# The experts' inner width in three parts (1024, 1024, 768 columns) in place of four quarters of 704

## What is computed

```python
def expert_choice_ffn(h, w_router, w_gate, w_up, w_down):   # D_MODEL 1024, EXPERT_FF 2816, N_EXPERTS 16
    ...
    cap = CAPACITY_FACTOR * n // N_EXPERTS                  # 32 tokens of one group, 64 of the other
    aff = jax.nn.softmax((t @ w_router).astype(jnp.float32), axis=-1)
    gate, idx = lax.top_k(aff.T, cap)
    def expert(args):
        wg, wu, wd, ix, g = args
        xe = t[ix]
        he = jax.nn.silu(xe @ wg) * (xe @ wu)
        return (he @ wd) * g[:, None].astype(he.dtype)
    ...
    y = jnp.zeros((n, D), h.dtype).at[idx.reshape(-1)].add(ye.reshape(-1, D))
```

## Time and profile before

| | us |
|---|---|
| median of 3 runs | 2247.36 |
| the profiled execution's own time | 2247.78 |
| its span, first to last instruction | 2246.0 |
| TensorE busy in the span | 2154.8 (96%) |
| VectorE busy | 1586.4 (71%) |
| ScalarE busy | 1373.0 (61%) |
| weight loads (PEld) recorded busy | 1873.9 (83%) |

### The profile page before, as it was taken

The page is one execution under the profiler, slowest core; times in us unless marked ns, Lnnn a source line. Parts: engine busy times, 40 slices in busy tenths (PEclk is TensorE's granted clock), DMA queues, the critical chain, the costliest instruction groups (busy, mean ns, idle before and its releaser), DMA issues.

```text
span 2246.0 us, 30582 instructions
## 1 busy us (share of the span) xinstructions
PE 2154.8 (96%) x11924; PEld 1873.9 (83%) x11924; DVE 1586.4 (71%) x1264; ACT 1373.0 (61%) x1118; POOL 180.5 (8%) x140
## 2 busy tenths in 40 slices
PE   6989979999995999999999999999999999999997
PEld 5857868888775898999988899898998989999896
DVE  5375334223447888888888888888888888888885
ACT  4364335222224677776777767677776777777774
POOL 1202200000013000010100101010010100101000
PEclk9999979999996999999999999999999999999999
DMA  5110142112415999999999999999999999999994
GB/s 228 57 56 25 57 134 70 62 57 113 162 67 205 362 380 353 386 365 370 375 368 372 367 378 374 367 377 365 378 366 375 369 358 391 359 373 372 366 382 173
DMA packets 71582, 623.99 MB, mean 278 GB/s; under 512 B 8336, under 2 KB 8720, under 8 KB 18800
## 3 DMA queue, kind: packets, MB, share of 16 engines
q1 hardware_dynamic: 63264, 595.62, 68.7%
q0 software_dynamic: 7840, 27.40, 4.3%
q10 hardware_dynamic: 432, 0.34, 0.0%
HBM read 609.70 MB, written 13.63 MB: 278 GB/s over the span
## 4 chain that ended last, share of the span: by engine, by line
PE 86%; DVE 5%; ACT 3%; issue 3%; DMA 2%; POOL 0%; ACTq 0%; DVEq 0%; POOLq 0%
PE PS L492 26%; PE PS L494 26%; PE PS L493 26%; DVE x_w_low L1114 2%; ACT x_w_high L1047 2%; PE PS L589 2%; PE PS L574 1%; PE PS L833 1%; PE PS L602 1%; PE PS L501 1%; DVE hidden L1465 1%; DMA bias_windows<-in_bias_prompt 1%; DVE s L1221 0%; ACT w_high L852 0%; PE PS L700 0%
## 5 line engine op out<-in xcount | busy, mean ns | idle before, releaser
L1114 DVE TENSOR_TENSOR x_w_low<-x_w_raw,x_w_high 128x2816 fp32r<-128x2816 f32 (+1 forms) x382 | 1176.6, 3090 | 244.0 <-ACT x_w_high L1047 242.4
L1047 ACT ACTIVATE x_w_high<-x_w_raw 128x2816 fp32r<-128x2816 f32 (+2 forms) x384 | 978.7, 2557 | 251.8 <-PE PS L494 212.0
L492 PE MATMUL PS<-x_w_high,xT_high 128*96 128x352 f32 x2048 | 667.9, 326 | 1.4 <-DVE xT_low L1114 1.4
L494 PE MATMUL PS<-x_w_high,xT_low 128*96 128x352 f32 x2048 | 660.7, 323 | 0.0
L493 PE MATMUL PS<-x_w_low,xT_high 128*96 128x352 f32 x2048 | 658.3, 321 | 0.0
L492 PEld LDWEIGHTS PS<-x_w_high,xT_high 128*96 128x96 f32 x2048 | 330.7, 161 | 6.8 <-issue 4.4
L493 PEld LDWEIGHTS PS<-x_w_low,xT_high 128*96 128x96 f32 x2048 | 332.9, 163 | 2.4
L494 PEld LDWEIGHTS PS<-x_w_high,xT_low 128*96 128x96 f32 x2048 | 332.3, 162 | 1.4
L492 PE MATMUL PS<-x_w_high,hidden_high 128*96 128x512 f32 x704 | 280.3, 398 | 2.2 <-DVE x_w_low L1114 1.1
L493 PE MATMUL PS<-x_w_low,hidden_high 128*96 128x512 f32 x704 | 278.4, 395 | 0.0
L494 PE MATMUL PS<-x_w_high,hidden_low 128*96 128x512 f32 x704 | 278.0, 395 | 0.0
(11 more groups left out here) (182 smaller groups left out, 1745.8 us busy)
## 6 DMA issues: line engine op xcount, KB each, us to landing
x_w_raw<-in_w_expert_gate SPq DMA_DIRECT2D x128, 1408.0 KB, 8.3
x_w_raw<-in_w_expert_up SPq DMA_DIRECT2D x128, 1408.0 KB, 8.8
x_w_raw<-in_w_expert_down SPq DMA_DIRECT2D x96, 1536.0 KB, 8.4
x_w_raw<-in_w_expert_down SPq DMA_DIRECT2D x32, 1024.0 KB, 6.9
w_raw<-in_w_in SPq DMA_DIRECT2D x20, 1024.0 KB, 4.8
x<-in_x_sample SPq DMA_DIRECT2D x8, 512.0 KB, 13.6
bias_windows<-in_bias_sample POOLq DMA_DIRECT2D x8, 512.0 KB, 3.7
w_raw<-in_w_out SPq DMA_DIRECT2D x4, 1024.0 KB, 4.8
```

The source lines that it names most:

```text
L492: mm(out, sh, mh, start=first, stop=False)
L494: return mm(out, sl, mh, start=False, stop=last)
L1047: a_(xh[:, w % SPLITS, 0:n], xraw[:, w % RAWS, 0:n], ACT.Copy).then_inc(x_high, 1)
L1114: return v.tensor_tensor(out, src, high.bitcast(F32), ALU.subtract)
```

## The change

Inner width is cut in parts of 1024, 1024 and 768 columns. A gate or up unit holds 3, 3 and 2 row blocks of 1024 columns in the first two parts, and 4 and 4 row blocks of 768 columns in the third. Each row block is multiplied in 512 + 512 or 512 + 256 columns. Down units hold 3, 3, 2 blocks for the first two parts and 3, 3 for the third; the sums of the down products build up over the three parts. There are again 24 units, in the order gate 0, up 0, gate 1, up 1, down 0, gate 2, up 2, down 1, down 2. The split `hidden` has two buffers, one for even and one for odd parts. TensorE turns part 0 in the places after the first and second unit of gate 1, part 1 after the first and second unit of down 0, part 2 after the first and second of down 1. Silu and the multiply run three times per expert in place of four. The core of the diff:

```diff
-HF = FF // 2
-QF = FF // 4
-QC = QF // 2
-FT = HF // P
+PARTS = [(0, 1024), (1024, 1024), (2048, 768)]
+PF = 1024
+FT = PF // P
...
+KT = {0: [(0, 3), (3, 3), (6, 2)], 1: [(0, 3), (3, 3), (6, 2)], 2: [(0, 4), (4, 4)]}
+DT = {0: [(0, 3), (3, 3), (6, 2)], 1: [(0, 3), (3, 3), (6, 2)], 2: [(0, 3), (3, 3)]}
 XU = []
-for _q in range(4):
-    XU += [("gate", _q, 0), ("gate", _q, 1)]
-    if _q == 2:
-        XU += [("down", 0, _c) for _c in range(4)]
-    XU += [("up", _q, 0), ("up", _q, 1)]
-XU += [("down", 1, _c) for _c in range(4)]
+for _kind, _q in (("gate", 0), ("up", 0), ("gate", 1), ("up", 1), ("down", 0), ("gate", 2), ("up", 2), ("down", 1), ("down", 2)):
+    XU += [(_kind, _q, _c) for _c in range(len((DT if _kind == "down" else KT)[_q]))]
...
-DT = [(0, 2), (2, 3), (5, 3), (8, 3)]
-HR = [(0, 5), (5, 3), (8, 3)]
+HR = {0: [(0, 4), (4, 4)], 1: [(0, 4), (4, 4)], 2: [(0, 3), (3, 3)]}
...
-MISC = {after("gate", 1): [("hidden", 0)], after("gate", 2, 0): [("hidden", 1)], after("gate", 2): [("hidden", 2)],
-        after("gate", 3, 0): [("hidden", 3)], after("up", 3): [("tokens", 0)],
-        after("down", 1, 0): [("hidden", 4)], after("down", 1, 1): [("hidden", 5), ("tokens", 1)]}
+MISC = {after("gate", 1, 0): [("hidden", 0)], after("gate", 1, 1): [("hidden", 1)],
+        after("down", 0, 0): [("hidden", 2)], after("down", 0, 1): [("hidden", 3)],
+        after("up", 2, 1): [("tokens", 0)], after("down", 1, 0): [("hidden", 4)],
+        after("down", 1, 1): [("hidden", 5)], after("down", 1, 2): [("tokens", 1)]}
...
+        def halves(q):
+            return [(0, 512), (512, PARTS[q][1] - 512)]
+        def hidden_round(j):
+            return [(q, *r) for q in range(3) for r in HR[q]][j]
...
-                        for k in range(4):
-                            for half in range(2):
-                                cols = slice(half * QC, (half + 1) * QC)
-                                i = split_product(PS[0:CAP, b0 + half, 0:QC], xT[0][:, 4 * c + k, :],
-                                                  xT[1][:, 4 * c + k, :], uh[:, k, cols], ul[:, k, cols],
-                                                  c == 0 and k == 0, c == 1 and k == 3)
+                        for k in range(nk):
+                            for half, (h0, hn) in enumerate(halves(q)):
+                                cols = slice(h0, h0 + hn)
+                                i = split_product(PS[0:CAP, b0 + half, 0:hn], xT[0][:, k0 + k, :],
+                                                  xT[1][:, k0 + k, :], uh[:, k, cols], ul[:, k, cols],
+                                                  k0 + k == 0, k0 + k == KD - 1)
...
-                            h, r = divmod(j, 3)
-                            f0, nf = HR[r]
-                            need = 2 * h + (1 if (f0 + nf) * P <= QF else 2)
-                            pe.wait_ge(S("x", "hidden"), e * 4 + need)
+                            part, f0, nf = hidden_round(j)
+                            pe.wait_ge(S("x", "hidden"), e * 3 + part + 1)
...
-                        h0 = (q % 2) * QF
-                        v.tensor_tensor(hid[:, h0:h0 + QF].rearrange("p (h f) -> p h f", h=2),
-                                        sg.rearrange("p (h f) -> p h f", h=2), PS[0:CAP, 2:4, 0:QC], ALU.mult
+                        w = PARTS[q][1]
+                        v.tensor_tensor(hid[:, 0:w], sg[:, 0:w], up_sums[:, 0:w], ALU.mult
                                         ).then_inc(S("x", "hidden"), 1)
```

More of the change, by code:

```diff
@@ L198, in encoder @@
         xTl = at("xT_low", 26304, KD * CAP, dt=F32R)
[L199 to L200 removed]
+        hidh = at("hidden_high", 48192, 2 * FT * CAP, dt=F32R).rearrange("p (b n) -> p b n", b=2)
+        hidl = at("hidden_low", 49728, 2 * FT * CAP, dt=F32R).rearrange("p (b n) -> p b n", b=2)
         ye = at("y_rows", 30208, D, CAP)
@@ L203, in encoder @@
         xe = at("gathered", 44736, D, CAP)
-        hid = at("hidden", 45760, HF, CAP)
-        sg = at("silu", 47168, QF, CAP)
+        hid = at("hidden", 45760, PF, CAP)
+        sg = at("silu", 46784, PF, CAP)
         ident = cst[:, C_ID:C_ID + 128]
@@ L232, in encoder @@
         PS = ctx.enter_context(nc.psum_tensor("PS", [P, 8, 512], F32))
+        gate_sums = PS[0:CAP, 0:2, :].rearrange("p b n -> p (b n)")
+        up_sums = PS[0:CAP, 2:4, :].rearrange("p b n -> p (b n)")
         t_dram = nc.dram_tensor("t_dram", [N, D], F32, kind="Internal").ap()
@@ L312, in unit_width, with unit_source @@
         def unit_width(w):
-            return DT[XU[w][2]][1] * D if XU[w][0] == "down" else 4 * QF
+            kind, q, c = XU[w]
+            return DT[q][c][1] * D if kind == "down" else KT[q][c][1] * PARTS[q][1]
+        def unit_source(e, w):
+            kind, q, c = XU[w]
+            n = unit_width(w)
+            at0 = sum(unit_width(i) for i in range(NXU) if XU[i][0] == kind and XU[i][1:] < (q, c))
+            src = {"gate": w_expert_gate, "up": w_expert_up, "down": w_expert_down}[kind]
+            return src[e, P * at0:P * (at0 + n)].rearrange("(p n) -> p n", p=P)
+        def halves(q):
+            return [(0, 512), (512, PARTS[q][1] - 512)]
+        def hidden_round(j):
+            return [(q, *r) for q in range(3) for r in HR[q]][j]
         block = ctx.enter_context(nc.Block())
@@ L364, in _ @@
                     b = w % RAWS
[L365 to L372, removed]
+                    sp.dma_start(xraw[:, b, 0:unit_width(w)], unit_source(e, w)).then_inc(x_loaded[b], 16)
         @block.gpsimd
@@ L789, in _ @@
             xT = [a.rearrange("p (k s) -> p k s", k=KD) for a in (xTh, xTl)]
-            hT = [a.rearrange("p (f s) -> p f s", f=FT) for a in (hidh, hidl)]
+            hT = [a.rearrange("p b (f s) -> p b f s", f=FT) for a in (hidh, hidl)]
             with pe.Fori(0, E) as e:
@@ L795, in _ @@
                     if kind == "down":
-                        f0, nf = DT[c]
+                        f0, nf = DT[q][c]
                         uh, ul = (a[:, b, 0:nf * D].rearrange("p (f d) -> p f d", f=nf) for a in (xh, xl))
-                        last_round = [r for r, (r0, rn) in enumerate(HR) if r0 < f0 + nf][-1]
-                        pe.wait_ge(S("x", "misc_read"), e * NU + PRE + use_no("hidden", 3 * q + last_round) + 1)
+                        last_round = [r for r, (r0, rn) in enumerate(HR[q]) if r0 < f0 + nf][-1]
+                        pe.wait_ge(S("x", "misc_read"), e * NU + PRE + use_no("hidden", 2 * q + last_round) + 1)
                         for f in range(nf):
@@ L804, in _ @@
                                 cols = slice(half * 512, (half + 1) * 512)
[L805 removed]
+                                i = split_product(PS[0:CAP, 4 + half, :], hT[0][:, q % 2, g, :], hT[1][:, q % 2, g, :],
                                                   uh[:, f, cols], ul[:, f, cols], q == 0 and g == 0,
[L807 removed]
+                                                  q == 2 and g == 5)
                     else:
[L809 removed]
+                        k0, nk = KT[q][c]
+                        uh, ul = (a[:, b, 0:unit_width(w)].rearrange("p (k f) -> p k f", k=nk) for a in (xh, xl))
                         if kind == "gate" and c == 0 and q > 0:
[L811 removed]
+                            pe.wait_ge(S("x", "silu"), e * 3 + q)
                         b0 = 0 if kind == "gate" else 2
[L813 to L818 removed]
+                        for k in range(nk):
[4 more added lines that the diff above has]
+                                                  k0 + k == 0, k0 + k == KD - 1)
                     i.then_inc(x_used, 1)
@@ L1059, in misc_high @@
                 act.wait_ge(S("x", "misc"), n)
-                c0, w = (j * 4 * CAP, 4 * CAP) if what == "tokens" else (HR[j % 3][0] * CAP, HR[j % 3][1] * CAP)
-                dst = xTh if what == "tokens" else hidh
+                if what == "tokens":
+                    dst, c0, w = xTh, j * 4 * CAP, 4 * CAP
+                else:
+                    part, f0, nf = hidden_round(j)
+                    dst, c0, w = hidh[:, part % 2, :], f0 * CAP, nf * CAP
                 a_(dst[:, c0:c0 + w], PS[:, bank, 0:w], ACT.Copy).then_inc(S("x", "misc_high"), 1)
@@ L1076, in expert_body @@
                     kind, q, c = XU[u]
-                    if kind == "gate" and c == 1:
+                    if kind == "gate" and c == len(KT[q]) - 1:
                         act.wait_ge(x_used, e * NXU + u + 1 + SPLITS)
                         if q > 0:
-                            act.wait_ge(S("x", "hidden"), e * 4 + q)
-                        a_(sg.rearrange("p (h f) -> p h f", h=2), PS[0:CAP, 0:2, 0:QC], ACT.Silu
-                           ).then_inc(S("x", "silu"), 1)
+                            act.wait_ge(S("x", "hidden"), e * 3 + q)
+                        w = PARTS[q][1]
+                        a_(sg[:, 0:w], gate_sums[:, 0:w], ACT.Silu).then_inc(S("x", "silu"), 1)
                     for what, j in MISC.get(u, []):
@@ L1447, in misc_low @@
```

(24 more changed lines are left out.)

2 lines of the change are left out of this document (1 added, 1 removed).

## The result

Changed kernel: 2258.82 us (median of 5, 2255.06 to 2260.85) against 2247.36 before on the same chip, ratio 1.0047 [1.0033, 1.0062]: slower by 0.5%. The forecast was 2253. The profiled execution took 2255.46 us, with a span of 2253.6, 7.7 us above that of before; it is the second fastest of the five.

A forecast was written before the change was run, and what follows sets the result against it. TensorE's own stream was taken as the bound, DMA just behind. Per expert 61.18 + 30.56 + 2.49 + 0.16 + 1.20 = 95.59 us against 95.24, +5.6 us for 16 experts, gave 2253 us; range 2236 to 2283.

The forecast's parts named there:

- Products: Gate and up products: 0.2315 us per 512 columns, 0.117 per 256; 61.18 us per expert against 61.44, 0.26 less.
- Rival 1: Gate and up products have a fixed cost; 512 columns start every 0.2267 us, 14 us less, 2239 us; chance 0.20.
- rival 2: Weights bound the 256-column gate and up products at 0.161 us each, 34 us more, 2287 us; chance 0.10.
- Handoff: TensorE waits 0.60 us for `hidden` of parts 0 and 1, twice per expert: 1.20 us lost.
- Waits that go: TensorE's waits of 0.26 us before the transposes and 0.33 us in the down products, per expert, vanish.
- the 0.16 carried over as unexplained: The 0.16 us of the 95.24 us per expert that products, transposes and two seen waits left over, kept in the sum.
- It is ready, with some 0.5 us to spare: Behind the handoff, VectorE's low part of a 3072 unit ends at 11.8 us; TensorE wants it at 12.4.
- Rival 3: Loads become the limit: late loads in every second handoff cost 22 us more, 2275 us; chance 0.15.
- Rival 3's reason: At a DMA share of 0.97 the expert stage may have no room for loads.
- The sum's own range: 2246 to 2261 us: 8 less if 256-column products cost 0.106 us, 8 more if the 0.5 us spare is used up.
- Splits: ScalarE's and VectorE's work on the 24 units per expert, 67,584 elements both times, stays unchanged to 0.1 us.

The follow-up runs named there:

- all_256: The changed kernel with all gate and up products 256 columns wide: 2272.44 us, 1.0113 of the kernel before.
- turn_later: The changed kernel with `hidden` of parts 0 and 1 turned one unit later: 2235.61 us, 0.9956 of the kernel before.
- six_buffers: The changed kernel with six raw buffers in place of four: 2248.38 us, 1.0009 of the kernel before.
- later_six: The changed kernel with `hidden` of parts 0 and 1 turned one unit later and six raw buffers: 2226.58 us, 0.9912 of the kernel before.
- all_128: The changed kernel with all gate and up products 128 columns wide: 3497.86 us (one run).

## Why the prediction was right, and what it mis-sized

The sign and the mechanism hold: widths nearly neutral, two handoffs that cost more than the widths give. Measured +11.5 us by medians (+7.7 by the profiled executions) against +5.6 forecast: the size was off by up to a factor of two.

- **Products.** 0.231 and 0.117 us, as taken; gate and up came to 61.0 in place of 61.18, mostly because 0.2315 was read from 28 distances and the mean over some 3000 is 0.231. Rival 1 (0.227) and rival 2 (0.161) did not happen, and all_256 shows both prices wrong.
- **Handoff.** 1.20 forecast, 1.31 measured, with 7.64 us of chain for 7.55. turn_later shows it by taking it away.
- **Waits that go.** They were 0.76, not 0.26 + 0.33: the 0.16 carried over as unexplained was mostly a third one (0.11) of the kernel before, and went too.
- **"It is ready, with some 0.5 us to spare".** At the places for which it was worked out, the first units of up 1 and gate 2, this held: by the trace after, VectorE's low part is done 0.5 us before TensorE asks, and no time is lost. The step that failed is that no other place was worked out: the first units of up 0 and gate 1, which stand behind a unit of 12 products as well, had no term in the sum, so late loads outside the handoffs were put at nothing. Their slack (by how much the low part is done before TensorE asks) is with loads in time 0.49 and 0.56 us (six_buffers), shorter than a late load (the earlier trace rows had 1.4 us each). It cost 0.54 us per expert, which six_buffers shows. In the kernel before, the 23 late up loads of the earlier trace rows were all of up 1, whose low parts were still done at least 0.8 us before TensorE began on them.
- **Rival 3 came in small.** It had priced 1.4 us per expert (0.7 for each handoff). At the handoffs a late load lengthened only the first one, and in two of 14 experts (to 0.95 and 1.07 us, where six_buffers has 0.72 throughout); the 0.54 came elsewhere. The sum's own range allowed 8 us for a used-up slack of 0.5 us, close to the 0.54 x 16 = 8.6 that came, but it meant other units: that closeness is luck.
- **Rival 3's reason fell.** The DMA engines were not at their limit at a share of 0.97: later_six moves 377 GB/s at the same share. What was short was the lead of the loads, one buffer beyond the three that the splits run ahead.
- **Splits.** ScalarE 981.0 and VectorE 1119.7 us in 14 periods for 982.9 and 1123.1: unchanged, as said. Loads of gate weights, now 1536 KB, landed after 8.8 us; for 1408 KB 8.3 stands in the earlier trace rows, and for 1536 KB 8.4.

The sum of the misses: -0.18 - 0.07 - 0.16 + 0.11 + 0.54 = +0.24 us per expert, on +0.35, which gives the 0.58 measured within 0.01.

What stays open: why the loads of up 0 come late in some experts and not in others. In the profiled execution the clusters with late up and gate loads begin at 900, 1188, 1762 and 2050 us, three periods apart or six. Nor is it shown why six_buffers still spreads over 6 us where later_six spreads over 3.

## What to carry to other kernels

When tiles get wider, work out for each handoff the chain of the slowest predecessor (here the split of the unit three ahead, in front of the multiply) against the work that the bound engine has until it asks, and move the asking by a unit where that is short: 23 us here, more than the widths were worth. A slack worked out with loads in time is no slack when the trace shows loads that come later than it is long; two more buffers bought it back. Compare the widths only after both, since a version judged with its first order of work (slower by 0.5%) was 0.9% faster with another.

## What the runs showed of the hardware

- In all_128 TensorE was recorded busy for 100 of 100 us from 900 us on, and the granted clock was 0.50 (1.2 GHz) all the same; from 840 to 880 us, with such products starting every 0.085 us in the stretch shown, it was 1.00 (2.4 GHz), and it changed between the two levels throughout the expert stage (0.50 from 720 to 820 us, 1.00 from 2000 to 2100), while TensorE was recorded busy for 2735 of its 2778 us. What sets it off no run here shows. Of the versions tried, only that with 128 columns met it: 3498 us at a clock of 0.75 over the span, for 2272 with 256 at 0.98.
- Products of 512 columns start every 0.231 us with 128x96 weights, and every 0.2267 with 128x128 in the stretch of the earlier trace rows (0.228 over all of the earlier stages). The 3 to 4 ns are not explained by any run here.
- A product's fixed cost in a stream is about 4 ns (all_256), near the 2.7 ns that the line through 352 and 512 left.
